# Layer 1's modulation chunks 3 to 5 move from the dense FFN to layer 1's mixer

## What is computed

```python
def first_block(x, c, ...):
    cond = jax.nn.silu(c)
    for layer in range(DEPTH):
        mod = (cond @ ada_w[layer] + ada_b[layer])[:, None, :]
        sh1, sc1, g1, sh2, sc2, g2 = jnp.split(mod, 6, axis=-1)
        h = rms_norm(x, norm_mix_g[layer]) * (1.0 + sc1) + sh1
        x = x + g1 * hybrid_mixer(h, positions, w_in[layer], ...)
        h = rms_norm(x, norm_ffn_g[layer]) * (1.0 + sc2) + sh2
        y = swiglu(h, ...) if layer % 2 == 0 else moe_swiglu(h, ...)
        x = x + g2 * y
    return rms_norm(x, final_g)
```

## Time and profile before

| | |
|---|---|
| median of 3 runs | 3063.79 us (3061.78 to 3063.87) |
| span of the profiled execution | 3061.6 us |
| PE busy | 2911.0 us (95%) |
| DVE busy | 1839.2 us (60%) |
| ACT busy | 1197.7 us (39%) |
| DMA, mean | 167 GB/s |

### The profile page before, as it was taken

How to read it: one execution, slowest core, us unless ns; L and a number is a source line. 1 busy time by engine, 2 the same in 40 slices (tenths; PEclk the granted TensorE clock), 3 DMA queues, 4 the chain that set the end, 5 groups by cost and what they waited for, 6 DMA issues and landing times.

```text
span 3061.6 us, 42645 instructions
## 1 busy us (share of the span) xinstructions
PE 2911.0 (95%) x17305; PEld 2502.0 (82%) x17305; DVE 1839.2 (60%) x2913; ACT 1197.7 (39%) x1723; POOL 0.2 (0%) x4
## 2 busy tenths in 40 slices
PE   7998998979999999899999999999999999989999
PEld 5888988879998666688887777788877888877998
DVE  4657886555556656577575465554547757656554
ACT  4344444443444445422223354422224222245544
POOL 0000000000000000000000000000000000000000
PEclk8999999989999999899999999999999999999999
DMA  9738983257767778355562222443434636422564
GB/s 308 255 118 258 270 264 124 83 159 208 227 179 292 283 294 320 109 166 165 144 186 72 73 70 56 125 143 112 138 102 141 199 110 182 128 80 81 149 180 128
DMA packets 557033, 511.40 MB, mean 167 GB/s; under 512 B 14307, under 2 KB 533542, under 8 KB 556710
## 3 DMA queue, kind: packets, MB, share of 16 engines
q1 hardware_dynamic: 477350, 390.56, 41.2%
q10 hardware_dynamic: 79488, 118.11, 11.8%
HBM read 507.57 MB, written 1.05 MB: 166 GB/s over the span
## 4 chain that ended last, share of the span: by engine, by line
PE 84%; ACT 5%; DVE 4%; DMA 4%; issue 2%; SPq 1%; ACTq 0%; DVEq 0%
PE bank L743 23%; PE bank L745 22%; PE bank L744 22%; PE bank L994 3%; DMA weights_raw<-in_moe_w 2%; PE bank L887 2%; ACT ring L1551 2%; DMA ada_halves<-in_ada_w 1%; PE bank L1449 1%; PE bank L1440 1%; PE bank L771 1%; PE bank L943 1%; PE bank L945 1%; PE bank L944 1%; DVE weights_split L2006 1%
## 5 line engine op out<-in xcount | busy, mean ns | idle before, releaser
L743 PE MATMUL bank<-hn_split,weights_split 128*128 128x256 f32 (+1 forms) x3008 | 1018.4, 339 | 69.7 <-DVE hn_split L2052 32.9
L744 PE MATMUL bank<-hn_split,weights_split 128*128 128x256 f32 (+1 forms) x3008 | 999.3, 332 | 0.0
L745 PE MATMUL bank<-hn_split,weights_split 128*128 128x256 f32 (+1 forms) x3008 | 998.8, 332 | 0.0
L2006 DVE TENSOR_TENSOR weights_split<-weights_raw,weights_split 128x1024 fp32r<-128x1024 f32 (+2 forms) x520 | 672.8, 1295 | 244.1 <-ACT weights_split L1497 243.8
L1497 ACT ACTIVATE weights_split<-weights_raw 128x1024 fp32r<-128x1024 f32 (+2 forms) x520 | 577.6, 1112 | 565.6 <-PE bank L745 514.5
L743 PEld LDWEIGHTS bank<-hn_split,weights_split 128*128 128x128 f32 x3008 | 585.2, 195 | 151.9 <-issue 80.0
L744 PEld LDWEIGHTS bank<-hn_split,weights_split 128*128 128x128 f32 x3008 | 585.6, 195 | 51.2 <-issue 1.9
L745 PEld LDWEIGHTS bank<-hn_split,weights_split 128*128 128x128 f32 x3008 | 584.3, 194 | 51.5
L743 PE MATMUL bank<-hidden_split,weights_split 128*128 128x256 f32 (+1 forms) x1144 | 382.3, 334 | 0.8 <-issue 0.8
L745 PE MATMUL bank<-hidden_split,weights_split 128*128 128x256 f32 (+1 forms) x1144 | 380.0, 332 | 0.0
L744 PE MATMUL bank<-hidden_split,weights_split 128*128 128x256 f32 (+1 forms) x1144 | 379.8, 332 | 0.0
(11 more groups left out here) (400 smaller groups left out, 2855.8 us busy)
## 6 DMA issues: line engine op xcount, KB each, us to landing
weights_raw<-in_w_ffn_in SPq DMA_DIRECT2D x176, 512.0 KB, 5.1
ada_halves<-in_w_ada ACTq DMA_DIRECT2D x96, 768.0 KB, 4.7
weights_raw<-in_moe_w SPq DMA_DIRECT2D x80, 704.0 KB, 6.7
ada_halves<-in_ada_w ACTq DMA_DIRECT2D x54, 768.0 KB, 5.8
weights_raw<-in_moe_w SPq DMA_DIRECT2D x66, 512.0 KB, 5.1
weights_raw<-in_w_in SPq DMA_DIRECT2D x60, 512.0 KB, 4.8
expert_down<-in_moe_w SPq DMA_DIRECT2D x25, 1024.0 KB, 5.1
weights_raw<-in_w_ffn_out SPq DMA_DIRECT2D x32, 768.0 KB, 4.8
```

What stands on the lines that cost most here:

```text
L743: mm(ps, wh, xh, start=first, stop=False)
L744: mm(ps, wh, xl, start=False, stop=False)
L745: return mm(ps, wl, xh, start=False, stop=last)
L2006: tt(split_view(slot, 1, kts, n), raw, split_view(slot, 0, kts, n).bitcast(F32), ALU.subtract)\
```

## The change

Class AdaTurns gets another user, named in1.1: one turn of 8 chunks (24 tiles of 128 columns) of layer 1's ada_w, columns 3072 to 6143. ffn1.0 keeps 12 tiles (4 chunks) in each of its two turns, columns 0 to 3071. In the mixer of layer 1 the quarters stand on DVE at the end of units 2 to 21 and 23 to 28, and behind the residuals of the first six units of out1.1; the groups on PE behind units 7, 11, 15, 19, 23, 28 and, counted on, 32 and 36 (the last unit of out1.1 is 36); ACT's DMA requests at the start and then behind units 4, 6, 8, 10, 12, 14, 16, 18, 20, 22, 25, 27, 29 and 31. The sums lie in the free end of the RAW slots, because the mixer uses their former place. The bias of the 24 columns is added after out1.1, ahead of the scale of the norm. The bookkeeping of vector_steps is rewritten without a change of what waits for what in the other phases. Number and kind of all instructions for the sums stay as they are.

```diff
-        FFN = {"ffn1.0": (2, 256, 24), ...
+        FFN = {"ffn1.0": (2, 256, 12), ...
...
+                if name == "in1.1":
+                    self.sums = [[RAW[:, i, 2048:2048 + ADA_COLS]] for i in range(2)]
+                    self.sum_at = [2 + q + (q >= 20) for q in range(4 * self.per)]
+                    self.load_at = [0 if q < 2 else self.sum_at[2 * q - 3] + 1 for q in range(2 * self.per)]
...
@@ PE, out1
+                if layer:
+                    ada_sums(0, ADA["in1.1"], 29)
+                    ada_sums(0, ADA["in1.1"], 30)
                 for m in range(2, KT):
                     pe.wait_ge(x_updated, XU[name] + m - 1)
                     pe.wait_ge(split_both, u0 + m + 1)
                     for k in order:
                         products(m, k)
+                    if layer:
+                        ada_sums(0, ADA["in1.1"], 29 + m)
...
@@ PE, mixer
+                    if layer and i < 28:
+                        ada_sums(0, ADA["in1.1"], i)
                     if i in extra:
                         extra[i]()
+                if layer:
+                    ada_sums(0, ADA["in1.1"], 28)
...
@@ ACT, out_phase and mixer
+                    if name == "out1.1":
+                        ada_parts(0, ADA["in1.1"], 30 + m)
...
+                if layer:
+                    ada_parts(0, ADA["in1.1"], 0)
...
                     if i in extra:
                         extra[i]()
+                    if layer and i:
+                        ada_parts(0, ADA["in1.1"], i)
...
@@ DVE
+            def mixer_sums(i):
+                for q, at_unit in enumerate(ADA["in1.1"].sum_at):
+                    if i == at_unit:
+                        sum_quarter(0, ADA["in1.1"], q)
...
                     if i in extra:
                         extra[i]()
+                    if layer:
+                        mixer_sums(i)
...
-                out_phase(f"out1.{layer}", T, lambda m, s: mod(2, m))
+                out_phase(f"out1.{layer}", T, lambda m, s: mod(2, m), (lambda m: mixer_sums(29 + m)) if layer else None)
+                if layer:
+                    x = ADA["in1.1"]
+                    dve.wait_ge(ada_done, x.done(0, x.per - 1))
+                    tt(MOD1[:, 72:96], PS[4][:, 0:24], col("ada_b", 72, 24), ALU.add).then_inc(mod_ready, 1)
+                    dve.wait_ge(mod_ready, x.mods + 1)
                 scale_columns(mod(4), col("norm_ffn_g", 8 * layer, 8), 0)
```

More of the change, by code:

```diff
@@ L448, in __init__ @@
             def __init__(self, name, chunks, tiles, mods, first):
-                self.name, (turns, T, self.n) = name, FFN[name]
-                self.conds = 1 if name == "ffn1.0" else 2
+                turns, _, self.n = FFN[name] if name in FFN else (1, SEQ, 24)
+                self.name, self.conds = name, 1 if name in ("ffn1.0", "in1.1") else 2
                 self.chunks, self.tiles, self.mods, self.first = chunks, tiles, mods, first
@@ L472, in program @@
         ADA, _chunks, _tiles, _mods, _first = {}, IN_CHUNKS, 48, 2, 0
[L473 to L479, removed]
+        for _n in ("ffn1.0", "in1.1", "ffn1.1", "ffna.0", "ffnb.0", "ffna.1"):
+            x = ADA[_n] = AdaTurns(_n, _chunks, _tiles, _mods, _first)
+            _chunks += x.n_turns * x.per
+            _tiles += x.n_turns * x.n
+            _mods += x.n_turns
+            _first += 0 if x.first_block else x.n_turns * x.n
         def raw_block(s, kts, n):
@@ L884, in ada_sums @@
                         for t in range(ADA_TILES):
[L885 removed]
+                            for s in range(x.conds_of(g, c)):
                                 at_col = x.conds * (ADA_TILES * c + t) + s
[L887 removed]
+                                i = mm(PS[4][:, at_col:at_col + 1], x.sums[c % 2][s][:, t * P:(t + 1) * P], tab("ones")[:, 0:1],
                                        start=True, stop=True)
@@ L2070, in residual @@
                 stt(X[:, m, c], ps, gate, X[:, m, c], ALU.mult, ALU.add).then_inc(x_updated, 1)
+            summed_at = [0, 0]
             def sum_quarter(g, x, q):
                 c, k0 = q // 4, q % 4 * 2
[L2075 to L2079, removed]
+                conds = x.conds_of(g, c)
                 for k in (k0, k0 + 1):
@@ L2085, in sum_quarter @@
                         dve.wait_ge(ada_done, x.done(g, c - 2))
-                    for s in range(x.conds):
-                        w, cond = AH[:, k // 4, k % 4, :], COND1[:, k:k + 1] if x.conds == 1 else COND2[:, k, s:s + 1]
+                    for s in range(conds):
+                        w, cond = AH[:, k // 4, k % 4, :], (COND1[:, k:k + 1] if x.first_block else COND2[:, k, s:s + 1])
+                        out = x.sums[c % 2][s][:, :]
                         if k == 0:
-                            i = ts(SUMS[c % 2][s][:, :], w, cond, None, ALU.mult)
+                            i = ts(out, w, cond, None, ALU.mult)
                         else:
-                            dve.wait_ge(*((ada_used, x.halves(g, c, 0) + 2) if k == 4 and s == x.conds - 1 else (vector_steps, step(k - 1, s))))
-                            i = stt(SUMS[c % 2][s][:, :], w, cond, SUMS[c % 2][s][:, :], ALU.mult, ALU.add)
-                        i.then_inc(ada_used if k % 4 == 3 and s == x.conds - 1 else vector_steps, 1)
+                            if k == 4 and s == conds - 1:
+                                dve.wait_ge(ada_used, x.halves(g, c, 0) + 2)
+                            else:
+                                dve.wait_ge(vector_steps, summed_at[s])
+                            i = stt(out, w, cond, out, ALU.mult, ALU.add)
+                        if k % 4 == 3 and s == conds - 1:
+                            i.then_inc(ada_used, 1)
+                        else:
+                            i.then_inc(vector_steps, 1)
+                            steps[0] += 1
+                            summed_at[s] = steps[0]
             def ffn(name, gate):
@@ L2355, in experts, with out_phase @@
                 dve.wait_ge(x_updated, x0 + KT * MOE_BLOCKS)
-            def out_phase(name, T, gate):
+            def mixer_sums(i):
+                for q, at_unit in enumerate(ADA["in1.1"].sum_at):
+                    if i == at_unit:
+                        sum_quarter(0, ADA["in1.1"], q)
+            def out_phase(name, T, gate, between=None):
                 u0, u1 = PH[name][0], ends[name][0]
```

15 lines of the change are left out of this document (9 added, 6 removed).

## The result

| | kernel before | changed kernel |
|---|---|---|
| median of the runs, us | 3063.83 | 3047.91 (3045.71 to 3050.94) |
| ratio to before, 95% interval | | 0.9946 [0.9934, 0.9958] |
| span of the profiled execution, us | 3061.6 | 3043.9 |

The changed kernel is 16 us faster. Run again beside other kernels it had 0.9946 [0.9933, 0.9959] and 0.9955 [0.9942, 0.9969]: 14 to 17 us. The forecast was 9.5 us (3054.3), its range ended at 3049.5. The direction was right, the gain was some 6 us larger.

What follows compares the result with a forecast made beforehand. PE was taken to bound the FFN, with DVE and DMA almost full and late modulation weights stalling it. FFN 15.5 us less, mixer and out1 6.0 more: 3063.8 - 9.5 = 3054.3 us, range 3049.5 to 3061.5.

Steps and rivals of the forecast that it cites:

- Groups, 5.4 us for 8: FFN: 8 groups of column sums leave PE's path at 0.67 us each, 5.4 us less.
- Waits for splits, 8.4, and the clock behind them, 1.7: FFN: PE's waits for DVE's weight splits between units go, 8.4 us, and half clock after one wait, 1.7 us.
- The half clock at the start: FFN's start: slow clock assumed to remain after the change, so no gain was counted for it.
- Unit 6, +1.1: Mixer: unit 6's quarter stands ahead of unit 9's split and delays PE's five products, 1.1 us more.
- Units 10 to 14 with group 3, +0.9: Mixer: five quarters ahead of the second rope, partly absorbed, with a group of column sums hidden beside; 0.9 us more.
- Groups 4 and 5, +1.3: Mixer: column sums behind units 19 and 23, where PE waits for nobody, 1.3 us more.
- Unit 28 and ACT's issue, +1.2 + 0.4: Mixer: unit 28's quarter ahead of gla_scale, 1.2 us more; ACT's DMA issue ahead of a split in unit 27, 0.4.
- out1, +1.1: Output projection: with a quarter per unit DVE becomes the bound for four or five units, 1.1 us more.
- Half clock in the mixer: Rival: new gaps before unit 9 and at out1's start bring 1.2 GHz stretches, 3.2 to 4.8 us more; chance 0.14.
- The FFN's waits stay: Rival: FFN splits are late because of weights_raw, so only the column sums are won, 3064.4 us; chance 0.06.
- Late halves in the mixer: Rival: halves land in 7 us in the mixer, late for units 12 to 20, 5 to 8 us more; chance 0.10.
- DVE as the mixer's bound: Rival: most mixer quarters stand in a chain, costing 30 us against 15.5, so slower at 3078 us; chance 0.08.

Runs made afterwards that it cites:

- e6_groups2: Changed kernel with each of the 8 groups of column sums left in the dense FFN issued twice; 3053.82 us, ratio to before 0.9970.
- e3_half_dma: Kernel before, each ada_w load in the dense FFN fetching two of four row tiles (384 KB for 768 KB); 3049.19 us, ratio 0.9961.
- b_copy: The kernel before, unaltered, run again for a second trace; 3063.52 us, ratio 0.9993.
- e2_mixer_only: FFN keeps 8 chunks a turn as in the kernel before; the changed kernel's mixer computes chunks 3 to 5 a second time; 3064.55 us, ratio 0.9999.
- e4_copy: Changed kernel with the FFN's ada_w halves asked for two units ahead, not four, second run of it; 3050.13 us, ratio to before 0.9957.
- e5_groups3: Changed kernel with each of the 8 groups of column sums left in the dense FFN issued three times; 3071.07 us, ratio to before 1.0027.
- t1_copy: Changed kernel with seven mixer quarters placed otherwise (units 6, 23 to 25 one unit earlier; 26 to 28 behind 25), second run; 3046.59 us, ratio to before 0.9943.
- e1_ffn_only: Changed kernel's FFN with the mixer of the kernel before; chunks 3 to 5 computed nowhere; 3044.72 us, ratio to before 0.9930.
- a_copy: The changed kernel, unaltered, run again for a second trace; 3048.15 us, ratio to before 0.9946.
- a_copy2: The changed kernel, unaltered, run once more in a later group; 3050.09 us, ratio to before 0.9955.

## Why the prediction was wrong in size

- **Groups, 5.4 us for 8.** Right: 5.1 in the trace of e6_groups2, 0.67 us apiece.
- **Waits for splits, 8.4, and the clock behind them, 1.7.** The mechanism was right, and e3_half_dma shows it alone. This is the term whose size failed: the step "6.9 us over 6 are between units" with "in the time of the slow part 1.7 us were lost" took what one trace of the kernel before showed for what the kernel does. Two more traces hold the same FFN. PE's waits for a split in b_copy and in e2_mixer_only, that at the stage's start (2.1 and 2.0 us) included, to be read against the 9.3 of the earlier trace rows:

```profile
PE bank L743 <- DVE weights_split L2006: 11.0, 8, 2.2
```

```profile
PE bank L751 <- DVE weights_split L2029: 10.3, 6, 2.7
```

  Between units that is 9.0 and 8.3 us where the first trace had 6.9. In the three traces nine such waits were longer than 1 us. A slow stretch came behind four of them (1.77 us in the first trace, 2.24 in b_copy, 2.06 and 2.69 in e2_mixer_only) and none behind the other five (1.22 to 2.24 us). So "after the longer wait it stayed at 1.00" was one draw, not a property of that wait. In the mean of the three the waits are 8.0 us for 6.9 and the stretches 1.3 for one, some 1.6 us more than was summed.
- **The half clock at the start.** The forecast had kept it on both sides of the sum ("plus the half clock at the start"). Here are 4 us from PE's first matmul of the stage, before and after:

```profile
244.90:248.90 4.00, 3.95 (x22) 3.98 (x23) 3.93 (x7) 1.36 (x2) 0.00 (x0) 0.62 0.33 94
```

```profile
244.50:248.50 4.00, 4.00 (x33) 4.00 (x34) 3.80 (x6) 2.23 (x4) 0.00 (x0) 1.00 0.36 104
```

  11 matmuls, about 1.4 us. It is not surely the change's. Six traces of 14 have it: the two of before, e3_half_dma, e4_copy, e5_groups3 and t1_copy; the three of the changed kernel don't, nor do e2_mixer_only and e1_ffn_only. Here it is in b_copy, and then the stretch behind its wait of 2.24 us, which lies across two windows:

```profile
248.00:252.00 4.00, 4.00 (x23) 4.00 (x23) 3.90 (x7) 1.27 (x3) 0.00 (x0) 0.57 0.62 180
308.00:312.00 4.00, 2.73 (x15) 2.76 (x16) 3.96 (x6) 1.26 (x2) 0.00 (x0) 0.73 1.01 285
312.00:316.00 4.00, 4.00 (x31) 4.00 (x31) 3.89 (x6) 1.81 (x3) 0.00 (x0) 0.84 0.95 312
```

  The mixer of b_copy began 4.0 us later than that of the first trace; 2.0 of that were there before the FFN's first matmul behind the opening wait (246.90 for 244.95), 2.1 arose in the FFN.
- **What else left the FFN.** 18.4 us in the stage less 15.5: the start's 1.4, two idle times of 0.42 us that the trace put down to issue (with 0.16 each, 1.2), and 0.3 that I can't place. Both idle times come back in e2_mixer_only, one of them in b_copy, and none in e3_half_dma, so they go with the late halves; the forecast put them at nothing and only let the upper bound of 16.5 hold them. From the first matmul behind the opening wait to the mixer's first copy the FFN takes 223.2, 225.3 and 223.5 us in the three traces with 8 chunks a turn, and 204.3, 204.9 and 204.8 in those of the changed kernel: 19.3 in the mean, which fits the 20 us of e1_ffn_only. The bound had been drawn as if every stretch and wait of one trace were all there are. The forecast's check on it didn't fit its sum either: two turns of 97.7 us and the half clock make over 195, more than the 193 that 15.5 us less leave. It had taken the 95.0 us of the dense expert for bare units, though two modulation chunks are in them. The changed FFN takes 95.2 us a turn with its four groups, 0.117 us a matmul once 0.67 is taken off for each group.
- **Unit 6, +1.1**: 0.86. **Units 10 to 14 with group 3, +0.9**: from there to the decayed scores and states the changed kernel is 0.7 us longer once the clock's stretches are taken off; whether the group shows there or the rope was not tried alone. **Groups 4 and 5, +1.3**: 0.81 + 0.67 by the same marks. **Unit 28 and ACT's issue, +1.2 + 0.4**: 1.18, and the DMA issue in unit 27 cost nothing visible. **out1, +1.1**: 0.7; from one residual to the next it takes 2.85 to 3.05 us (590.69, 593.74, 596.59, 599.64, 602.68) where it took 2.88. Sum 4.9 for 6.0; only the quarters of units 6 and 28 were moved to see their price, the others are read from the trace. **Behind out1, put at nothing:** from its last residual to the router's first matmul 6.08 us where it took 5.56, in all three traces of the changed kernel, +0.5. There the last group and the bias of the 24 columns now stand ahead of the norm's scale, which is the likely reason. So 5.4 for 6.0.
- **What came on top**: the block of the gla outputs, 1.45 us shorter after than before by the clock. It was so in all three traces of the changed kernel and in neither of the two of before, so it is not the luck of one execution, but no step of the forecast had it. With it the stretch is 4.0 us longer in the first trace; in a_copy and a_copy2 one slow stretch fewer early in the mixer leaves 2.4.
- **The rivals.** Half clock in the mixer: no; its granted clock was 0.95 and 0.96 (0.94 before). The page TensorE: Matmul & The Clock Gate of the Trainium skill (Why this matters for your kernels) warns of long idle gaps between bursts of matmuls. In these traces waits of 1.8 to 2.7 us were already followed by slow stretches, in four cases of nine, so the measured gaps count and not only long ones; and the change took away more of them in the FFN than it made in the mixer. The FFN's waits stay: no (e3_half_dma). Late halves in the mixer: no, they landed in 4.7 us and DVE never waited for them. DVE as the mixer's bound: no; it is busy 105.7 of 136.2 us, and of 26 quarters in the mixer two were shown bare (units 6 and 28).

Of the 6 us that were missing, about 3 are in the FFN: 1.2 in the issue gaps, the rest in the slow stretch at the start and in waits and stretches that the one trace of before undercounts. Some 0.6 are in the mixer's terms and 1.45 in the clock of the gla outputs. The remaining 1.5 us can't be placed; the part that both kernels share scatters by more. The places, the waits and their cause were right. The range ended too early because it took its bounds from one trace's waits and stretches. That the two errors of size, too small a gain and too large a cost, point the same way is why a gain of 16 lies outside it.

## What to carry to other kernels

Where a transfer, an engine of moderate load and a saturated PE stand in a chain, ask how long the transfer takes to land and how far ahead it is asked for: two units of lead (5.8 us) for 7 us of landing cost this kernel some 12 us, and moving half of the work to a stage with spare DMA and DVE time cost 1 to 5 us for a gain of 20. Price a PE stall with the half clock that may follow it, as a chance per stall taken from all of them and from more than one execution (here four stalls of nine), and give the range both ends of that count. Work put on DVE in a mixer of many small steps shows only where it stands ahead of a step that PE or ACT waits for: 1.18 and 0.86 us at two of 26 places, and at most 0.7 us for five others together.

## What the runs showed of the hardware

- Matmuls of one column in a row can be followed by a lower granted clock although PE isn't idle: 18 in a row (1.93 us) were followed by about 3.3 us at the 1.2 GHz level in 7 of 8 cases of one trace (e5_groups3), 12 in a row (1.26 us, e6_groups2) and 6 in a row (0.59 us, three traces of the changed kernel) in none in the FFN.
- The same instructions behind the same kind of wait get a slow stretch or not, from one execution to the next: of nine waits of 1.2 to 2.7 us in three traces of the same FFN four did, and a stretch costs 1.4 to 1.7 us. The block of the gla outputs took 11.51, 12.97 or 14.59 us in kernels whose mixers are the same. The page TensorE: Matmul & The Clock Gate of the Trainium skill (Part 1: The HAM clock gate) says of the start of a kernel that the number of slow matmuls varies from run to run; the traces show the same in the middle of one.
- A load of 768 KB took 7.0 us (median) to land at a DMA share of 0.9, 6.3 at 0.79 and 4.7 at 0.59; one of 384 KB 4.7 at 0.77.
